# A mixing sub-layer laid out anew: panel order, pooling and taps on VectorE, three weight slots

## What is computed

```python
h = rmsnorm(x, p['g_mix'])
z = h @ p['w_in']          # columns: u_pool 512 | ga 512 | gb 512 | gate_pool 1024 | gate_conv 1024
v = ga * jax.nn.sigmoid(gb)
y_pool = pool_mixer(u_pool, ...) @ p['w_pool_out']   # trailing means over 2/4/8/16 frames minus the frame,
                                                     # a 128x128 map per group of 128 channels, a scale
y_conv = conv_module(v, ...) @ p['w_conv_out']       # depthwise conv of width 31, LayerNorm, swish
merged = jax.nn.sigmoid(gate_pool) * y_pool + jax.nn.sigmoid(gate_conv) * y_conv
x = x + merged @ p['w_out']
x = x + hier_moe(rmsnorm(x, p['g_ffn']), ...)        # 32 experts, a coarse and a top-2 router
```

## Time and profile before

| | us |
|---|---|
| median of 3 runs | 1088.79 |
| lowest, highest | 1087.95, 1089.5 |
| the profiled execution's own time | 1090.29 |
| its span in the trace | 1088.5 |

### The profile page before, as it was taken

One profiled execution on the slowest core, in us unless ns is written; L12 is line 12 of the kernel. 1 busy time (PEld: TensorE's weight loads), 2 busy tenths in 40 slices (PEclk: granted clock), 3 DMA queues, 4 the chain that ended last, 5 costly groups with the idle time before them and its releaser, 6 DMA issues.

```text
span 1088.5 us, 15813 instructions
## 1 busy us (share of the span) xinstructions
PE 949.7 (87%) x6165; PEld 901.6 (83%) x6165; DVE 570.2 (52%) x752; ACT 297.2 (27%) x482; POOL 218.1 (20%) x159
## 2 busy tenths in 40 slices
PE   5799869795999989999899994699999999999910
PEld 5799869795999889999788884699999999999810
DVE  5312998689798673323431436244444444444448
ACT  6321211210111382212411321123333232323323
POOL 0008990025334000000000001212122222212000
PEclk9899979897999999999999996799999999999965
DMA  8021011101111102111131537669999999999157
GB/s 261 1 59 39 19 39 31 44 29 29 50 36 34 48 26 78 48 58 48 45 126 41 192 111 293 222 255 327 342 342 336 354 335 358 348 356 335 52 198 299
DMA packets 77740, 169.93 MB, mean 156 GB/s; under 512 B 10763, under 2 KB 48155, under 8 KB 68449
## 3 DMA queue, kind: packets, MB, share of 16 engines
q1 hardware_dynamic: 68481, 152.05, 39.6%
q0 software_dynamic: 9216, 17.32, 4.8%
HBM read 156.83 MB, written 22.47 MB: 165 GB/s over the span
## 4 chain that ended last, share of the span: by engine, by line
PE 73%; issue 12%; DVE 8%; ACT 3%; DMA 2%; POOL 1%; POOLq 0%; SPq 0%; DVEq 0%; ACTq 0%
PE ps L1348 29%; PE ps L1581 21%; PE ps L1521 9%; PE ps L1565 8%; PE ps L1551 2%; DVE x L1314 2%; POOL w_lo L583 1%; PE ps L1500 1%; DVE x L1325 1%; PE ps L1441 1%; DVE hT L1074 1%; PE ps L1358 1%; PE ps L1492 1%; DMA yy<-YK 1%; ACT C L785 1%
## 5 line engine op out<-in xcount | busy, mean ns | idle before, releaser
L1348 PE MATMUL ps<-hT,w_hi 128*128 128x352 f32 x1344 | 337.1, 333 | 35.0 <-POOL w_lo L583 17.6
L1348 PEld LDWEIGHTS ps<-hT,w_hi 128*128 128x128 f32 x1344 | 242.8, 195 | 37.2 <-issue 34.2
L1581 PEld LDWEIGHTS ps<-XT,wgu 128*128 128x128 f32 x2048 | 236.3, 194 | 5.2 <-ACT XT L853 2.6
L1581 PE MATMUL ps<-XT,wgu 128*128 128x104 f32 x2048 | 236.1, 277 | 2.2 <-ACT XT L853 2.2
L1348 PE MATMUL ps<-hT,w_lo 128*128 128x352 f32 x672 | 222.4, 331 | 0.0
L1348 PEld LDWEIGHTS ps<-hT,w_lo 128*128 128x128 f32 x672 | 130.1, 194 | 0.0
L999 DVE SCALAR_TENSOR_TENSOR C<-V,w_dw,C 128x1086 f32<-128x1086 f32 x80 | 111.1, 1459 | 0.2 <-issue 0.2
L1273 DVE TENSOR_TENSOR wdn_lo<-wdn,wdn_hi 128x1024 fp32r<-128x1024 f32 x64 | 75.5, 1221 | 54.0 <-ACT wdn_hi L875 54.0
L1521 PE MATMUL ps<-wo_hi,hT 128*128 128x512 f32 x288 | 92.6, 403 | 4.7 <-DVE hT L1074 4.5
L907 DVE TENSOR_TENSOR w_lo<-w_raw,w_hi 128x1024 fp32r<-128x1024 f32 (+1 forms) x30 | 37.7, 1258 | 105.8 <-ACT w_hi L670 105.8
L636 POOL DMA_INDIRECT YK<-Y,s_now x32 | 32.8, 1026 | 268.1 <-DVE Y L1247 268.1
(11 more groups left out here) (209 smaller groups left out, 1229.7 us busy)
## 6 DMA issues: line engine op xcount, KB each, us to landing
wgu<-in_w_gate SPq DMA_DIRECT2D x32, 1024.0 KB
wgu<-in_w_up SPq DMA_DIRECT2D x32, 1024.0 KB
wdn<-in_w_down SPq DMA_DIRECT2D x32, 1024.0 KB
w_raw<-in_w_in SPq DMA_DIRECT2D x28, 512.0 KB, 3.8
yy<-YK SPq DMA_DIRECT2D x8, 1024.0 KB, 12.2
xs<-in_x_prompt SPq DMA_DIRECT2D x8, 512.0 KB, 6.8
wo_raw<-in_w_out SPq DMA_DIRECT2D x8, 512.0 KB, 3.8
xr<-in_x_prompt SPq DMA_DIRECT2D x16, 256.0 KB, 2.8
```

Source lines behind the costliest of these rows:

```text
L1348: m = pe.matmul(ps[:, bank, 0:CH], a[:, s, w + k, :], r[:, w + k, c * CH:(c + 1) * CH], start=(k == 0 and q == 0), stop=(k == K - 1 and q ...
L1581: m = pe.matmul(ps[:, 2 + b, o:o + CAP], wgu[u][:, h, c, f * P:(f + 1) * P], XT[:, b, c, 0:CAP], start=(c == 0), stop=(c == KD - 1))
```

## The change

- **Panel order.** One list `PANELS` names 44 panels: four times (gb j, ga j, u 3-j), then gp 0, gp 1, then (po j, gp j+2), po 6, po 7, then all eight gate_conv panels gc, then all eight conv-out panels co. gp and po are gate_pool and pool-out. Every engine runs an unrolled loop over this list. The gate_conv values wait in `Gc` until their co panel.
- **Prologue.** Three panels' products (24 matmuls each) stand between the transposes instead of two; a product stands behind every transpose from the fifth on.
- **Weight slots.** Three slots (and a fourth used once). `w_lo` overwrites `w_raw`, and SP loads a slot when PE has done with it.
- **POOL** has no work in the mixing sub-layer. The pooling goes to DVE in `pool_group`, its rounding `d_hi` to ACT, and all `w_lo` to DVE.
- **Taps.** `taps(n)` takes the next n taps of the ready group that was tapped longest ago; a table says how many in each panel.
- **Group map.** Its twelve chunk products stand one by one behind products of panels 5, 8, 12 and 13, in banks 6 and 7.
- **LayerNorm** sums stand between the products of gc 2 to gc 5, the taps must be done by then, and ACT takes sigmoid, root and swish in turn.
- **Output.** `M` is split as each part is merged, all quarters of `w_out` have places of their own, and PE takes the first seven of eight parts of two results before the last part is needed.

The core of the diff:

```diff
+        W_AT = [(r_w + s * 4096, r_w + 12288 + s * 4096) for s in range(3)] + [(r_x, r_s + 4096)]
+        w_raw = [at(f"w_raw{s}", [P, KD, P], F32, a) for s, (a, b) in enumerate(W_AT)]
+        w_lo = [at(f"w_lo{s}", [P, KD, P], F32R, a) for s, (a, b) in enumerate(W_AT)]
+        w_hi = [at(f"w_hi{s}", [P, KD, P], F32R, b) for s, (a, b) in enumerate(W_AT)]
...
+        PANELS = []
+        for j in range(GR):
+            PANELS += [("gb", j), ("ga", j), ("u", GR - 1 - j)]
+        PANELS += [("gp", 0), ("gp", 1)]
+        for j in range(KD - 2):
+            PANELS += [("po", j), ("gp", j + 2)]
+        PANELS += [("po", KD - 2), ("po", KD - 1)]
+        PANELS += [("gc", j) for j in range(KD)] + [("co", j) for j in range(KD)]
+        NPAN = len(PANELS)
+        AT_PANEL = {p: m for m, p in enumerate(PANELS)}
+        FIRST = 3
...
+        def slot_of(m):
+            return m if m <= FIRST else (m - FIRST - 1) % 3
+
+        def slot_before(m):
+            return m - 4 if m < 7 else m - 3
...
+            def panel_load(m):
+                s, K = slot_of(m), depth(m)
+                if m > FIRST:
+                    sp.wait_ge(s_mm, mm_count(slot_before(m), 2))
+                sp.dma_start(w_raw[s][:, 0:K], panel_source(m)).then_inc(s_w[s], 16)
...
+            for m in range(FIRST + 1, NPAN):
+                panel_load(m)
...
-            for g in range(GR):
-                w = 2 << g
-                src = U[:, g, :]
-                for k in range(g + 1):
-                    lag, lo = 1 << k, (2 << k) - 1
-                    link(pool.tensor_tensor(win[:, k % 2, lo:UW], src[:, lo:UW], src[:, lo - lag:UW - lag], ALU.add))
-                    src = win[:, k % 2, :]
...
-                link(pool.tensor_copy(d_hi[:, g, :], diff[:]))
-                link(pool.tensor_tensor(d_lo[:, g, :], diff[:], d_hi[:, g, :].bitcast(F32), ALU.subtract))
-                pool.sem_inc(s_diff, 1)
...
-            def split_lo(n, s, K):
-                pool.wait_ge(s_whi, n + 1)
-                pool.tensor_tensor(w_lo[:, s, 0:K], w_raw[:, s, 0:K], w_hi[:, s, 0:K].bitcast(F32),
-                                   ALU.subtract).then_inc(s_wlo, 1)
...
+            LN0 = AT_PANEL[("gc", 2)]
+            for m in range(FIRST, NPAN):
+                kind, j = PANELS[m]
+                if m + 1 < NPAN:
+                    split_hi(m + 1)
+                for c in range(CHUNKS):
+                    if kind in BY_ACT:
+                        evict(m, c)
...
+                    if m in (5, 8, 12):
+                        group_hi({5: 0, 8: 3, 12: 6}[m] + c)
...
+                    if (m, c) == (LN0, 2):
+                        ln_square(0)
+                    if (m, c) == (LN0 + 1, 0):
+                        ln_root(0)
+                        ln_square(1)
+                    if (m, c) == (LN0 + 1, 1):
+                        swish(0)
...
+            def taps(count):
+
+                for _ in range(count):
+                    g = min(range(ready[0]), key=lambda g: (next_tap[g] == CW, last_tap[g]))
+                    k = next_tap[g]
...
+            def pool_group(m):
+
+                g = PANELS[m][1]
+                w = 2 << g
+                dve.wait_ge(s_evA, EV_A[(m, 2)])
+                src = U[:, g, :]
+                for k in range(g + 1):
+                    lag, lo = 1 << k, (2 << k) - 1
+                    link(dve.tensor_tensor(win[:, k % 2, lo:UW], src[:, lo:UW], src[:, lo - lag:UW - lag], ALU.add))
+                    src = win[:, k % 2, :]
+                dve.tensor_tensor(diff[:, 0:w - 1], src[:, PH:PH + w - 1], inv_cnt[:, 0:w - 1], ALU.mult).then_inc(s_pool, 1)
+                pooled[0] += 1
+                dve.scalar_tensor_tensor(out=diff[:, w - 1:SEQ], in0=src[:, PH + w - 1:PH + SEQ], scalar=1.0 / w,
+                                         in1=U[:, g, PH + w - 1:PH + SEQ], op0=ALU.mult, op1=ALU.subtract)
+                dve.wait_ge(s_pool, pooled[0])
+                dve.tensor_tensor(diff[:, 0:w - 1], diff[:, 0:w - 1], U[:, g, PH:PH + w - 1], ALU.subtract)
...
-            def later_taps(i, jj):
-                k0 = A_TAPS + sum(B_TAPS) * i
-                for k in range(jj * B_TAPS[0], jj * B_TAPS[0] + B_TAPS[jj]):
-                    taps(k0, k, GR * (k0 + k - 1))
...
+            TAPS = {3: 2, 4: 6, 6: 2, 7: 7, 9: 2, 10: 7, 14: 3, 15: 5, LN0 - 2: 6, LN0 - 1: 7, LN0: 3}
+            for m in range(FIRST, NPAN):
+                kind, j = PANELS[m]
+                before = PANELS[m - 1][0]
+                if before == "ga":
...
+                        glu(m - 1, c)
+                    ready[0] += 1
+                if before == "po":
+                    gated(m - 1)
+                if before == "co":
+                    merged(m - 1)
...
+                if m + 1 < NPAN:
+                    split_lo(m + 1)
+                if m in (4, 7, 10):
+                    diff_lo(m // 3 - 1)
+                if m in (3, 6, 9, 12):
+                    pool_group(m - 1)
...
+                if 16 <= m <= 27:
+                    taps(3 if kind == "po" else 6)
...
+                if kind == "co" and j >= 2:
+                    m_lo(j - 2)
...
+            m_lo(KD - 2)
+            wo_split_lo(0, 2)
+            merged(LAST_CO)
+            wo_split_lo(0, 3)
+            for c in range(CHUNKS):
...
+            MEAN_AFTER = {(LN0, 1): 0, (LN0, 2): 1, (LN0 + 1, 1): 2, (LN0 + 2, 0): 3}
+            VAR_AFTER = {(LN0 + 1, 0): 0, (LN0 + 1, 2): 1, (LN0 + 2, 1): 2, (LN0 + 3, 0): 3}
+            GROUPS_AFTER = {(5, 0): (0,), (5, 1): (1,), (5, 2): (2,), (8, 0): (3,), (8, 1): (4,), (8, 2): (5,),
+                            (12, 0): (6,), (12, 1): (7,), (12, 2): (8,), (13, 0): (9, 10), (13, 1): (11,)}
...
+                    wait_evicted(pe, m - 2, c)
+                    product(m, c, hi, lo)
+                    for i in GROUPS_AFTER.get((m, c), ()):
+                        grouped(i)
...
+            def out_part(n, ks):
...
+                for k in ks:
+                    if n < 2:
+                        pe.wait_ge(s_mlo, k + 1 if k < KD - 1 else KD - 1 + min(CHUNKS, ((t + 1) * P + CH - 1) // CH))
+                    if n == 2 and k == KD - 1:
+                        pe.wait_ge(s_mlo, KD - 1 + CHUNKS)
+                    if t == 0:
+                        pe.wait_ge(s_wolo, 4 * h + k // 2 + 1)
...
+            for n in range(2):
+                wait_evicted(pe, LAST_CO - 1, n)
+                out_part(n, range(KD - 1))
```

876 lines of the change are left out of this document (443 added, 433 removed).

## The result

The changed kernel takes 1020.54 us (median of 4 runs, 1019.68 to 1020.66), the kernel before 1088.37 us beside it (4 runs, 1087.08 to 1089.5). The ratio is 0.9375, with a 95% interval of 0.9363 to 0.9386: faster by 67.8 us. The forecast was 1025 us, with a range of 1018 to 1039. The profiled execution took 1020.66 us with a span of 1018.8 us.

The account below looks back on a forecast made before the run. PE was taken to bound the kernel up to 530.6 us, with 69.2 us lost. An output projection 59.2 us earlier plus 4.4 us made 63.6 us, span 1088.5 to 1024.9 us, forecast 1025 us, range 1018 to 1039.

Parts of the forecast that it names:

- The start of the output projection: PE reaches the output projection at 471.4 us, 59.2 us earlier, from 8.2 + 453.2 + 8.2 + 1.8 us.
- Part 1: Panels' waits for w_lo: DVE makes each w_lo a panel ahead, 2.8 us in, with margins of 8.9 or 3.0 us.
- The two margins of 2.3 us: Time to spare at two hand-offs: y_lo before the first pool-out panel, and all 124 taps before the first LayerNorm sum.
- I count no wait there: Pairs and triples: DVE has 15.4 of 17.5 us and 34.7 of 36.5 us of work, so PE waits for nothing.
- a small w_lo stands behind long work, or beside it: Old kernel's panels: one cause for both kinds of PE wait, 17.6 us for POOL's w_lo and one of 12.7 us.
- Part 2: Prologue: products cover transpose waits, six instead of four done by the history; 8.2 us lost and 1.8 us slow pace stay.
- Part 3: LayerNorm: PE's gaps go (2.8 us for a_lo and others); ACT, with 16 table loads, has 46.3 us of work in 58.6.
- Part 4: Output projection's start: 4.1 us of wait and 2 us of slow pace go, a 1.7 us wait comes; gain 4.4 us.
- the missed margins: Rival at two hand-offs with 2.3 us each: misses of 3 to 4 us cost 10 to 12 us, 1036 us; chance 0.16.
- the slow taps: Rival on DVE: taps stay slow for reasons other than POOL; at 3.0 us each, 1213 us; chance 0.03.
- the tables: Rival in LayerNorm: ACT table loads take twice 1.30 us, 67 us of work in 58.6, giving 1029 us; chance 0.05.
- the prologue: Rival: a third 512 KB load delays the transposes, up to two products (7.8 us) stay put, 1033 us; chance 0.08.

Follow-up runs that it names:

- e_pool_early: Changed kernel plus 56 idle GpSimd adds of 128x384, one behind the other, from panel 4 on over the triples gb, ga, u: 1030.54 us.
- e_lumps_gpsimd: Changed kernel with the taps of panels 16 to 27 in three lumps (18, 18, 15) and w_lo of panels 15 to 27 on GpSimd: 1048.72 us.
- e_wlo_gpsimd: Changed kernel with w_lo of the 13 panels 15 to 27 (pairs gate_pool and pool-out) made by GpSimd again: 1020.83 us.
- e_old_prologue: Changed kernel with the prologue's transposes of tiles 5 and 6 together again and the product between them later, on PE alone: 1030.11 us.
- e_plain_start: Changed kernel with the output projection taking its first two results whole, without seven parts of each ahead: 1020.36 us.

## Why the prediction was right, and where its sizes were off

The sign, the mechanism and the place of nearly all the gain came as worked out, though it leans on a part that did nothing (the seven parts ahead) and on a room in DVE's list that was larger than its sum. By its own steps:

- **The start of the output projection**: 467.75 us for 471.4. No step that sets this sum failed; 3.65 us are sizes. A matmul of a panel takes 143.1 / 888 = 0.161 us for 0.162, over 2484 of them 2.7 us. The LayerNorm sums are eight matmuls in 1.63 us, 13.0 us in all for 15.7; the products beside them run at 4.08 us for 3.9 and give 1.8 us of that back. The first product starts at 19.52 us for 19.9 and takes 5.34 us for 5.68. These make 4.3 us; 0.7 us went the other way in small pieces that weren't taken apart.
- **Part 1**: right, no wait. The two margins of 2.3 us were 2.3 us (the last tap ends at 342.0, the sum starts at 344.3) and about 2.5 us (y_lo ends at 194.0, pool-out 0 starts near 196.6). No run tests these two. Another hand-off, y_lo in the second triple, gave way in e_pool_early: with half a microsecond more on a tap PE waits 7.3 us there. "I count no wait there" came true for the triples with more room than I had given it: DVE is busy for 29.0 to 31.3 us of a triple, and I had 34.7 of 36.5. Of before's two kinds of waits I wrote "a small w_lo stands behind long work, or beside it"; e_lumps_gpsimd shows that beside is no better than behind when w_lo comes amid the lump, and e_wlo_gpsimd that the engine doesn't matter in the pairs once the lumps are gone. The slow taps beside POOL are shown too, and for the 12.7 us wait of before they weigh as much as the lump: 14.3 us of its 29.0. What the change owes to "GpSimd out" is nothing in the pairs as far as w_lo goes; what it owes to it in the triples was not run.
- **Part 2**: six products by the history, no wait, as forecast; e_old_prologue costs 9.6 us, but part of that is the mismatch of its lists and not the worth of the part.
- **Part 3**: ACT kept up, with 16 table loads of 1.283 us each. The time by the Trainium skill's figure (page ScalarE: Activation LUTs, section What ACT_TABLE_LOAD costs, about 2.66 us) was a rival, and the trace decided for the row (the load at 379.93 us is followed by the root at 381.23, 1.30 us on). The gates-first order carries the LayerNorm stage, with 16 us of margin.
- **Part 4**: the term that was most mis-sized. I had 4.4 us; the stretch from there to the end fell from 557.9 to 551.05 us, 6.8 us. The waits fell by 3.15 us (4.31 in before, 1.16 now; I had 2.4), the first 18 matmuls took 4.33 us for 5.15 (I had nothing there), and the slow pace of 2.1 us went as forecast. That is 6.1 of the 6.8 us; the rest is in the stops' own cost and 0.3 us behind the router's start. The mechanism I gave was wrong in one point: not the seven parts of two results cover M (e_plain_start, without them, takes 1020.36 us), but the order on DVE and the wait for wo_lo ahead of it.
- **Rivals**: the missed margins, the slow taps, the tables and the prologue each had their row to watch, and none came.

The sum: 62.9 us ahead of the output projection for 59.2, and 6.8 us behind it for 4.4, together 69.7 us for 63.6. That is the 1018.8 us span for 1024.9.

## What to carry to other kernels

Where two engines feed a third, look at the longest unbroken run of background work on either one before moving work between them: here a small operand was late by what was left of that run, on the same engine or on its neighbour, and moving it to the neighbour didn't help (1048.7 us for 1046.8) where cutting the run did (1020.5). Judge a spread by the room that the waits for the next operand show on the busy engine, and test it by adding idle work beside it. And once an order of one engine's list is tuned, the others' lists are tied to it: a swap uncovers their waits too.

## What the hardware showed that I had not expected

- A row of DVE taps held a GpSimd subtraction that came amid it back to its end (12.35 us for 2.39, 7.91 us for 1.29), at no cost to the taps (1.27 us each). GpSimd adds that were already running when the row began got in between the taps and made them 1.85 us each. The moment goes with it and not the size: an add of 384 elements that came 3.05 us into a row was held too (4.02 us).
- The price of a short wait is not its length: 18.9 us of waits in three cost 26.3 us and one of 6.9 us cost 8.9, through the pace behind them. Seven stops of 3.9 us in all cost 5.8 us at a granted clock of 1.00, about 0.3 us a stop on top.
- A gain of 1.85 us of PE time was gone 60 us later, where the granted clock fell earlier. That early fall stands in five of fourteen traces with the same code there, most of them without an earlier start.
